# Two feed-forward chores exchanged between VectorE and GpSimd: weight sums of the down projection and sums of its activations

## The chip, the cores and the metric

The kernel runs on one core of a Trainium2 chip. The metric is device time in microseconds (us) of one execution; lower is better. TensorE does the matrix products, VectorE (DVE) and GpSimd (POOL) element-wise work, ScalarE (ACT) activations; SyncE (SP) issues the weight loads.

## The reference

Two transformer-like blocks of two layers each, in float32, on 256 tokens of width 1024. Between mixers (which the change leaves alone) stand six feed-forward stages, of which only these lines matter:

```python
# first block, 2 layers: d_ff = 4096
h @ mlp_w1  ->  square(relu(.))  ->  @ mlp_w2
# second block, 2 layers, two stages each: d_ff = 2816
(jax.nn.silu(h @ w_gate) * (h @ w_up)) @ w_down
```

So there are two plain stages and four gated ones, each with one or two projections in and one projection down.

## The kernel before

All weights are one stream of units of 128x1024 float32 (512 KB), loaded by SP into `ring`, which has 12 slots; TensorE hands slots back through `freed`, and SP then loads the next unit.

Each feed-forward (`Ffn`, `pe_ffn`, `act_ffn`, `dve_ffn`, `pool_ffn`) is a Strassen-like scheme with 7 products in place of 8 and has three parts.

- **Lead.** Four tiles of the hidden layer are computed directly.
- **Job phase.** Each job takes two ring units and makes seven products of 4 matmuls each. Four of its left operands are sums of weight blocks, which `in_sums` writes into `b.sums` (`HELD` = 4 buffers) with four instructions of 128x512: VectorE does the even jobs, GpSimd the odd ones. After each pair of hidden tiles (one job in a plain stage, two in a gated one) ScalarE copies one product out of PSUM (L543), VectorE joins the products (`join`, L584 to L593), in a gated stage ScalarE applies the SiLU (L550), and VectorE writes the activations to `hid_all` (L611 plain, L607 gated).
- **Down phase.** It goes over 16 pairs of hidden tiles (plain) or 11 (gated), 76 in all. Each pair takes two ring units, has seven products (`part` 1 to 7), and needs two things prepared. The *weight sums* (`down_sums`, four instructions of 128x512, L419, L420, L422, L424) go into the next of the same four `b.sums` buffers. The *inner-tile sums*, called activation sums here (four instructions of 128x128, L664, L665, L667, L669), go into `x_sums` in `cat`, also four buffers. A buffer comes free for pair p when TensorE has finished pair p - 4, counted by `job_done`.

TensorE asks for both before each pair, in `take`:

```python
def take(p):
    pe.wait_ge(*fn.summed(k, fn.jobs + p))          # weight sums
    pe.wait_ge(k.hid_summed, fn.down0 + p + 1)      # activation sums
```

The order of its work in the down phase is written out by hand. It first takes pairs 0 and 1 and runs parts 1, 6 and 5 of both, which need no bank that VectorE is still joining; then it waits for the last `joined`, and does parts 2, 3, 7, 4 of both. The middle pairs are done one after another. The last four pairs (`TAIL` = 4) are taken one after another with only part 1 between two takes; the other parts follow, each for all four pairs, so that the joins of the output can begin early.

Every engine works through its own queue in program order; semaphores are the only coupling.

Of the kernel before, what the change touches and what calls it, by code (L numbers as in the profile page):

```python
# [14 lines left out]
ALU = mybir.AluOpType  # L15
# [59 lines left out]
LEAD, TAIL, HELD = 4, 4, 4  # L75
# [23 lines left out]
class Steps:  # L99
# [5 lines left out]
    def __init__(self, sem, labels):  # L105
        labels = labels.split() if isinstance(labels, str) else labels
        assert len(set(labels)) == len(labels)
        self.sem, self.labels, self.marked = sem, labels, 0
# [27 lines left out]
def bc(ap, n):  # L136

    return ap.unsqueeze(1).to_broadcast([ap.shape[0], n, ap.shape[1]])
# [130 lines left out]
def half(tt):  # L269
    return slice(tt * P, tt * P + P)  # L270
# [80 lines left out]
class Ffn:  # L351
# [6 lines left out]
    def __init__(self, n):  # L358
        before = [self.shape(i) for i in range(n)]
        self.gated, self.tiles, self.ins, self.pairs, self.jobs, self.downs = self.shape(n)  # L360
        self.n, self.units = n, FFN_UNITS[n]
        self.lead0 = LEAD * n
        self.hid0 = sum(x[1] for x in before)
        self.job0 = sum(x[4] + x[5] for x in before)
        self.dve0 = sum(x[4] // 2 + x[5] for x in before)
        self.pool0 = sum(x[4] // 2 for x in before)
        self.down0 = sum(x[5] for x in before)
        self.pair0 = sum(x[3] for x in before)
        self.silu0 = sum(x[3] for x in before if x[0])
# [8 lines left out]
    def summed(self, k, i):  # L378

        if i >= self.jobs:  # L380
            return k.dve_summed, self.dve0 + self.jobs // 2 + i - self.jobs + 1
        return (k.pool_summed, self.pool0 + i // 2 + 1) if i % 2 else (k.dve_summed, self.dve0 + i // 2 + 1)

    def joined(self, i):
# [4 lines left out]
def unit_halves(k, eng, fn, i):  # L389

    out = []
    for j in range(2):
        u = fn.units + LEAD * fn.ins + 2 * i + j
        eng.wait_ge(k.filled[u % RING], 16 * (u // RING + 1))
        out += [k.ring[:, u % RING, 0:512], k.ring[:, u % RING, 512:1024]]
    return out


def in_sums(k, b, eng, fn, i, done):

    s = b.sums[:, i % HELD, :, :]
    if i >= HELD:
        eng.wait_ge(k.job_done, fn.job0 + i - HELD + 1)
    a11, a12, a21, a22 = unit_halves(k, eng, fn, i)
    eng.tensor_tensor(s[:, 0, :], a21, a22, ALU.add)  # L405
    eng.tensor_tensor(s[:, 2, :], a11, a21, ALU.subtract)
    eng.drain()
    eng.tensor_tensor(s[:, 1, :], s[:, 0, :], a11, ALU.subtract)
    eng.drain()
    eng.tensor_tensor(s[:, 3, :], a12, s[:, 1, :], ALU.subtract).then_inc(done, 1)  # L410


def down_sums(k, b, eng, fn, p, done):

    i = fn.jobs + p
    s = b.sums[:, i % HELD, :, :]
    eng.wait_ge(k.job_done, fn.job0 + i - HELD + 1)
    b11, b12, b21, b22 = unit_halves(k, eng, fn, i)
    eng.tensor_tensor(s[:, 0, :], b12, b11, ALU.subtract)  # L419
    eng.tensor_tensor(s[:, 2, :], b22, b12, ALU.subtract)  # L420
    eng.drain()
    eng.tensor_tensor(s[:, 1, :], b22, s[:, 0, :], ALU.subtract)  # L422
    eng.drain()
    eng.tensor_tensor(s[:, 3, :], s[:, 1, :], b21, ALU.subtract).then_inc(done, 1)  # L424
# [131 lines left out]
def dve_ffn(k, b, dve, fn, n_in, before_pairs=None):  # L556
    low, high = half(0), half(1)
    b11, b12, b21, b22 = k.h[:, 0:4, low], k.h[:, 0:4, high], k.h[:, 4:8, low], k.h[:, 4:8, high]
    hs = k.h_sums

    dve.wait_ge(k.h_low, 2 * n_in + 2)
    dve.drain()
    dve.tensor_tensor(hs[:, 0, :, :], b12, b11, ALU.subtract)
    dve.tensor_tensor(hs[:, 2, :, :], b22, b12, ALU.subtract)
    dve.drain()
    dve.tensor_tensor(hs[:, 1, :, :], b22, hs[:, 0, :, :], ALU.subtract)
    dve.drain()
    dve.tensor_tensor(hs[:, 3, :, :], hs[:, 1, :, :], b21, ALU.subtract).then_inc(k.tokens_summed, 1)
    in_sums(k, b, dve, fn, 0, k.dve_summed)
    for f in range(LEAD):  # L570
        dve.wait_ge(k.act_ready, fn.lead0 + f + 1)
        dve.tensor_tensor(b.hid_all[:, f, :], k.bank(4 + f)[:, int(fn.gated), :], k.hid_act[:, f % 2, :],
                          ALU.mult).then_inc(k.hid_ready, 1)
    in_sums(k, b, dve, fn, 2, k.dve_summed)
    if before_pairs is not None:
        before_pairs()

    def join(q):

        pre, i = b.pre[q % 2], q * fn.ins  # L580
        dve.wait_ge(k.first_copied, fn.pair0 + q + 1)
        for j in range(fn.ins):
            got, c = k.regions[:, (i + j) % 4, :, :], pre[:, j, :, :]
            dve.tensor_tensor(c[:, 0:5:4, :], bc(c[:, 7, :], 2), got[:, 1:3, :], ALU.add)  # L584
        dve.drain()
        for j in range(fn.ins):
            got, c = k.regions[:, (i + j) % 4, :, :], pre[:, j, :, :]
            dve.tensor_tensor(c[:, 5:7, :], bc(c[:, 4, :], 2), got[:, 4:6, :], ALU.add)
        dve.drain()
        for j in range(fn.ins):  # L590
            got, c = k.regions[:, (i + j) % 4, :, :], pre[:, j, :, :]
            dve.tensor_tensor(c[:, 1:4:2, :], c[:, 5:7, :], got[:, 3:5, :], ALU.add)
            last = dve.tensor_tensor(c[:, 2, :], c[:, 6, :], got[:, 6, :], ALU.subtract)  # L593
        last.then_inc(k.joined, 1)

    down = 0
    for q in range(fn.pairs):
        pre, f = b.pre[q % 2], LEAD + 2 * q
        out = b.hid_all[:, f:f + 2, :].rearrange("p n (h c) -> p (n h) c", c=P)
        join(q)  # L600
        ahead = (q + 1) * fn.ins + HELD
        for i in range(ahead - fn.ins, min(ahead, fn.jobs)):
            if i % 2 == 0:
                in_sums(k, b, dve, fn, i, k.dve_summed)
        if fn.gated:
            dve.wait_ge(k.silu_ready, fn.silu0 + q + 1)
            dve.tensor_tensor(out, k.silu[q % 2].rearrange("p (s c) -> p s c", c=P), pre[:, 1, 0:4, :],  # L607
                              ALU.mult).then_inc(k.hid_ready, 2)
        else:
            dve.drain()  # L610
            dve.scalar_tensor_tensor(out, pre[:, 0, 0:4, :], 0.0, pre[:, 0, 0:4, :], ALU.max, ALU.mult).then_inc(  # L611
                k.hid_ready, 2)
        while down < ahead - fn.jobs:
            down_sums(k, b, dve, fn, down, k.dve_summed)
            down += 1
    for p in range(down, fn.downs):
        down_sums(k, b, dve, fn, p, k.dve_summed)


def dve_join_first(k, dve, fn):  # L620
# [29 lines left out]


def pool_ffn(k, b, pool, fn, n_in):
    low, high = half(0), half(1)

    pool.wait_ge(k.y_done, 2 * n_in + 2)
    for i in range(1, fn.jobs, 2):
        in_sums(k, b, pool, fn, i, k.pool_summed)
    for p in range(fn.downs):
        x = k.x_sums[:, p % HELD, :, :]
        if p >= HELD:  # L660
            pool.wait_ge(k.job_done, fn.job0 + fn.jobs + p - HELD + 1)
        pool.wait_ge(k.hid_ready, fn.hid0 + 2 * p + 2)
        f1, f2 = b.hid_all[:, 2 * p, :], b.hid_all[:, 2 * p + 1, :]
        pool.tensor_tensor(x[:, 0, :], f1[:, high], f2[:, high], ALU.add)  # L664
        pool.tensor_tensor(x[:, 2, :], f1[:, low], f1[:, high], ALU.subtract)  # L665
        pool.drain()
        pool.tensor_tensor(x[:, 1, :], x[:, 0, :], f1[:, low], ALU.subtract)  # L667
        pool.drain()
        pool.tensor_tensor(x[:, 3, :], f2[:, low], x[:, 1, :], ALU.subtract).then_inc(k.hid_summed, 1)  # L669


def act_root_table(k, act):
# [572 lines left out]
def second_vector(k, s, dve, w):  # L1245
# [52 lines left out]
    for l in range(LAYERS):  # L1298
# [3 lines left out]
        dve.tensor_tensor(s.sg_wt.rearrange("p (h t) -> p h t", h=4), s.p("sg_w").rearrange("p (h t) -> p h t", h=4),  # L1302
                          bc(k.c("tril_st"), 4), ALU.mult)
        dve_ffn(k, s, dve, Ffn(2 + 2 * l), border(1, l, 0) - 1)
        dve_boundary(k, s, dve, 3 * l, "mix_pre_g", None, Ffn(2 + 2 * l))

# [167 lines left out]
        out_normed(1, 4)  # L1474
        dve_boundary(k, s, dve, 3 * l + 1, "ffn2_pre_g", lambda: out_gated(1))
        dve_ffn(k, s, dve, Ffn(3 + 2 * l), border(1, l, 1))
        if l < LAYERS - 1:
            dve.wait_ge(s.params, (l + 2) * 16)
# [1312 lines left out]
def tail_vector(k, f, s, dve, w, layer):  # L2791
    def norm(which, gain, bias):
# [3 lines left out]
        for tt in range(2):  # L2796
# [24 lines left out]
            last.then_inc(k.h_high, 1)  # L2821
    norm(LN1, "ln1_g", "ln1_b")
    dve_ffn(k, f, dve, Ffn(layer), border(0, layer, LN1), lambda: dve.wait_ge(f.residual, 2 * (2 * layer) + 2))
    norm(LN2, "ln2_g", "ln2_b")
    n = border(0, layer, PLE)
# [315 lines left out]
```

## Time and profile before

| | |
|---|---|
| time, median of 3 runs (lowest to highest) | 2066.53 us (2061.09 to 2070.67) |
| time of the profiled execution | 2056.4 us |
| its span, first to last instruction | 2054.6 us |
| mean granted TensorE clock | 0.984 of full speed |
| busy: PE, DVE, ACT, POOL | 98%, 53%, 17%, 31% of the span |
| chain that ended last | PE 92%, DVE 4%, ACT 1%, POOL 0% |

A busy share says how long an engine had an instruction running, not whether somebody waited for it. The chain that ended last is followed back from the last instruction, so an engine with a large share there sets the time. Shares are averages over unlike stages; what an exchange of work in one phase costs is read from the timeline of that phase. Each float32 matmul of the source appears as two records, so a down pair has 14 matmul records and a job 56.

### The profile page before, as it was taken

To read this page: it belongs to the slowest core of one execution; us is meant where nothing else is said; L and a number is where in the kernel's file an instruction comes from. 1 tells how busy PE (TensorE), PEld (TensorE's weight loads), DVE (VectorE), ACT (ScalarE), POOL (GpSimd) and SP (SyncE) were. 2 spreads that over 40 slices of the span, in tenths; PEclk is the share of its full clock that TensorE was granted. 3 is DMA by queue.
4 is the path that set the end of the run, shared out by engine and by line. 5 is a ranking of instruction groups with operands and counts; after the bars stand their busy time and mean duration, and the time that the engine had idled before them with its cause. 6 is when DMAs were issued, how large, how long until landed. Compare 5 with 4: busy or idle time off the path is not lost.

```text
span 2054.6 us, 31876 instructions
## 1 busy us (share of the span) xinstructions
PE 2004.0 (98%) x12016; PEld 1549.2 (75%) x12016; DVE 1088.1 (53%) x1959; ACT 345.4 (17%) x772; POOL 636.9 (31%) x665
## 2 busy tenths in 40 slices
PE   8999999999999999999999999999999999999998
PEld 6875995468769944699658869994899478869973
DVE  4343866434638655346636544665456636444564
ACT  1332000012420000300024511000200025310000
POOL 0000644310106453134412603434234405312342
PEclk9999999999999999999999989999999999989999
DMA  8422544443144444354435116544744344025453
GB/s 312 142 68 73 191 174 168 147 152 128 56 146 172 164 179 159 120 203 170 164 133 164 53 34 199 174 148 143 268 172 175 145 155 143 11 93 185 166 180 117
DMA packets 82935, 305.46 MB, mean 149 GB/s; under 512 B 9264, under 2 KB 9392, under 8 KB 82416
## 3 DMA queue, kind: packets, MB, share of 16 engines
q1 hardware_dynamic: 80496, 294.93, 40.9%
q0 software_dynamic: 2304, 8.65, 1.2%
q8 instruction: 95, 1.56, 0.3%
q14 instruction: 40, 0.33, 0.1%
HBM read 302.23 MB, written 1.05 MB: 148 GB/s over the span
## 4 chain that ended last, share of the span: by engine, by line
PE 92%; DVE 4%; ACT 1%; DVEq 1%; issue 1%; DMA 0%; POOL 0%; ACTq 0%; SPq 0%
PE psum L439 26%; PE psum L478 21%; PE psum L242 9%; PE psum L867 8%; PE psum L1814 6%; PE psum L2363 4%; PE psum L315 4%; PE psum L302 3%; PE psum L454 3%; PE psum L326 3%; PE psum L1673 1%; PE psum L451 1%; PE psum L283 1%; PE psum L2738 1%; PE psum L1751 0%
## 5 line engine op out<-in xcount | busy, mean ns | idle before, releaser
L439 PE MATMUL psum<-sq,space 128*128 128x128 f32 x2400 | 302.7, 276 | 0.0
L439 PEld LDWEIGHTS psum<-sq,space 128*128 128x128 f32 x2400 | 286.2, 193 | 0.0
L478 PE MATMUL psum<-space,cat 128*128 128x512 f32 x456 | 208.2, 592 | 0.0
L242 PE MATMUL psum<-h,ring 128*128 128x256 f32 x864 | 195.4, 386 | 7.0 <-DMA ring<-in_weights 7.0
L242 PEld LDWEIGHTS psum<-h,ring 128*128 128x128 f32 x864 | 166.7, 194 | 32.6 <-issue 9.7
L478 PEld LDWEIGHTS psum<-space,cat 128*128 128x128 f32 x456 | 86.4, 189 | 109.3 <-issue 109.3
L405 POOL TENSOR_TENSOR space<-ring 128x512 f32<-128x512 f32 x50 | 66.3, 1326 | 316.7 <-PE psum L439 265.4
L478 PE MATMUL psum<-ring,space 128*128 128x512 f32 x304 | 144.2, 594 | 6.8 <-DVE space L424 6.8
L664 POOL TENSOR_TENSOR cat<-space 128x128 f32<-128x128 f32 x76 | 59.6, 784 | 213.3 <-PE psum L478 213.3
L439 PE MATMUL psum<-sq,ring 128*128 128x128 f32 x800 | 107.7, 278 | 9.1 <-DVE space L410 9.1
L478 PEld LDWEIGHTS psum<-ring,space 128*128 128x128 f32 x304 | 56.7, 189 | 78.7 <-issue 66.4
L419 DVE TENSOR_TENSOR space<-ring 128x512 f32<-128x512 f32 x76 | 55.5, 731 | 107.9 <-PE psum L478 107.9
L439 PE MATMUL psum<-h,space 128*128 128x128 f32 x800 | 107.0, 277 | 0.0
L439 PEld LDWEIGHTS psum<-sq,ring 128*128 128x128 f32 x800 | 99.0, 195 | 9.4 <-DVE space L410 9.4
L439 PE MATMUL psum<-h,ring 128*128 128x128 f32 x800 | 105.7, 275 | 0.0
L584 DVE TENSOR_TENSOR tmp<-tmp,psum 128x256 f32<-128x256 f32 x68 | 26.8, 419 | 141.4 <-ACT tmp L543 141.3
L439 PEld LDWEIGHTS psum<-h,space 128*128 128x128 f32 x800 | 98.8, 194 | 0.0
L302 PEld LDWEIGHTS psum<-h,ring 128*128 128x128 f32 x832 | 94.6, 192 | 4.6 <-issue 1.9
L439 PEld LDWEIGHTS psum<-h,ring 128*128 128x128 f32 x800 | 97.4, 192 | 0.0
L302 PE MATMUL psum<-h,ring 128*128 128x128 f32 x832 | 96.1, 275 | 0.0
L315 PE MATMUL psum<-h,ring 128*128 128x128 f32 x832 | 94.4, 275 | 0.0
L315 PEld LDWEIGHTS psum<-h,ring 128*128 128x128 f32 x832 | 93.6, 192 | 0.0
(411 smaller groups left out, 3302.8 us busy)
## 6 DMA issues: line engine op xcount, KB each, us to landing
ring<-in_weights SPq DMA_DIRECT2D x552, 512.0 KB, 4.1
space<-in_rows POOLq DMA_DIRECT2D x8, 512.0 KB, 8.5
space<-in_gains POOLq DMA_DIRECT2D x6, 512.0 KB, 4.3
const<-in_consts SPq DMA_DIRECT2D x1, 1493.0 KB, 11.0
h<-in_x SPq DMA_DIRECT2D x1, 1024.0 KB, 4.8
x<-in_x_tok SPq DMA_DIRECT2D x1, 1024.0 KB, 15.3
out<-x SPq DMA_DIRECT2D x2, 512.0 KB, 2.6
space<-in_params POOLq DMA_DIRECT2D x2, 509.5 KB, 7.0
```

Source lines behind the costliest of these rows:

```text
L242: last = pe.matmul(out, unit[:, i, :], rhs[:, i, :], start=(i == 0), stop=(i == KD - 1), skip_group_check=True)
L302: ins = pe.matmul(out[:, half(0)], unit[:, i, :], k.h[:, i, half(0)], start=(i == 0), stop=(i == KD - 1), skip_group_check=True)
L315: last = pe.matmul(out[:, half(1)], unit[:, i, :], k.h[:, i, half(1)], start=(i == 0), stop=(i == KD - 1), skip_group_check=True)
L326: ins = pe.matmul(k.psum[:, 2 * tt + b, :], lhs(j)[:, half(tt)], unit[:, b * 512:b * 512 + 512], start=first and j == 0, stop=last and j = ...
L405: eng.tensor_tensor(s[:, 0, :], a21, a22, ALU.add)
L439: last = pe.matmul(out, weights(i), tokens(i), start=(i == 0), stop=(i == 3), skip_group_check=True)
L454: pe.matmul(out[:, 0, :], a[:, j, :], k.h[:, j, low], start=False, stop=(j == 3), skip_group_check=True)
L478: return pe.matmul(k.psum[:, bank, :], lhs, rhs, start=(p == 0), stop=(p == fn.downs - 1), skip_group_check=True)
L664: pool.tensor_tensor(x[:, 0, :], f1[:, high], f2[:, high], ALU.add)
L867: return pe.matmul(out, lhsT, rhs, start=start, stop=stop, skip_group_check=True)
L1814: return pe.matmul(out, lhsT, rhs, start=start, stop=stop, skip_group_check=True)
L2363: return pe.matmul(out, lhsT, rhs, start=start, stop=stop, skip_group_check=True)
```

## The change

Before, VectorE makes the weight sums of the down phase and GpSimd the activation sums. After, GpSimd makes the weight sums and VectorE the activation sums. In `dve_ffn` the loop that interleaved `down_sums` with the last joins is gone; the activation sums of all pairs stand behind the loop over hidden pairs, so behind the last join and the last activation. In `pool_ffn` `down_sums` stands where the activation sums stood. The counts on which TensorE waits are moved from `dve_summed` to `pool_summed`. TensorE's and ScalarE's programs are otherwise the same.

```diff
@@ class Ffn
-        self.dve0 = sum(x[4] // 2 + x[5] for x in before)
-        self.pool0 = sum(x[4] // 2 for x in before)
+        self.dve0 = sum(x[4] // 2 for x in before)
+        self.pool0 = sum(x[4] // 2 + x[5] for x in before)
@@ def summed
-            return k.dve_summed, self.dve0 + self.jobs // 2 + i - self.jobs + 1
+            return k.pool_summed, self.pool0 + self.jobs // 2 + i - self.jobs + 1
@@ def dve_ffn
-    down = 0
     for q in range(fn.pairs):
...
-        while down < ahead - fn.jobs:
-            down_sums(k, b, dve, fn, down, k.dve_summed)
-            down += 1
-    for p in range(down, fn.downs):
-        down_sums(k, b, dve, fn, p, k.dve_summed)
+    for p in range(fn.downs):
+        x = k.x_sums[:, p % HELD, :, :]
+        if p >= HELD:
+            dve.wait_ge(k.job_done, fn.job0 + fn.jobs + p - HELD + 1)
+        dve.drain()
+        f1, f2 = b.hid_all[:, 2 * p, :], b.hid_all[:, 2 * p + 1, :]
+        dve.tensor_tensor(x[:, 0, :], f1[:, high], f2[:, high], ALU.add)
+        dve.tensor_tensor(x[:, 2, :], f1[:, low], f1[:, high], ALU.subtract)
+        dve.drain()
+        dve.tensor_tensor(x[:, 1, :], x[:, 0, :], f1[:, low], ALU.subtract)
+        dve.drain()
+        dve.tensor_tensor(x[:, 3, :], f2[:, low], x[:, 1, :], ALU.subtract).then_inc(k.hid_summed, 1)
@@ def pool_ffn
     for p in range(fn.downs):
-        x = k.x_sums[:, p % HELD, :, :]
...
-        pool.wait_ge(k.hid_ready, fn.hid0 + 2 * p + 2)
...
-        pool.tensor_tensor(x[:, 3, :], f2[:, low], x[:, 1, :], ALU.subtract).then_inc(k.hid_summed, 1)
+        down_sums(k, b, pool, fn, p, k.pool_summed)
```

On VectorE, the end of the first feed-forward's job phase before: the join and activation of the last hidden pair (waiting for ScalarE's copy), then the weight sums of down pair 3, those of pairs 0 to 2 standing further up between earlier joins.

```order
L584 TENSOR_TENSOR tmp<-tmp,psum 128x2x128 [waits strassen_first_copied]
L588 TENSOR_TENSOR tmp<-tmp,psum 128x256
L592 TENSOR_TENSOR tmp<-tmp,psum 128x2x128
L593 TENSOR_TENSOR tmp<-tmp,psum 128x128
L611 SCALAR_TENSOR_TENSOR space<-tmp 128x512
L419 TENSOR_TENSOR space<-ring 128x512 [waits ring_filled6,ring_filled5,strassen_products]
L420 TENSOR_TENSOR space<-ring 128x512
L422 TENSOR_TENSOR space<-ring,space 128x512
L424 TENSOR_TENSOR space<-space,ring 128x512
```

On VectorE at the same place of the changed kernel (where L610 is the former L611), the four activation sums of pair 0 follow that last activation:

```order
L584 TENSOR_TENSOR tmp<-tmp,psum 128x2x128 [waits strassen_first_copied]
L588 TENSOR_TENSOR tmp<-tmp,psum 128x256
L592 TENSOR_TENSOR tmp<-tmp,psum 128x2x128
L593 TENSOR_TENSOR tmp<-tmp,psum 128x128
L610 SCALAR_TENSOR_TENSOR space<-tmp 128x512
L618 TENSOR_TENSOR cat<-space 128x128
L619 TENSOR_TENSOR cat<-space 128x128
L621 TENSOR_TENSOR cat<-cat,space 128x128
L623 TENSOR_TENSOR cat<-space,cat 128x128
```

So the activation sums that TensorE needs first have moved from an engine that ran beside the joins to a place behind the last of them.

On GpSimd, before, the last of its job sums is followed by activation sums that wait for `hidden_ready`:

```order
L405 TENSOR_TENSOR space<-ring 128x512 [waits ring_filled10,ring_filled9,strassen_products]
L406 TENSOR_TENSOR space<-ring 128x512
L408 TENSOR_TENSOR space<-space,ring 128x512
L410 TENSOR_TENSOR space<-ring,space 128x512
L664 TENSOR_TENSOR cat<-space 128x128 [waits hidden_ready]
L665 TENSOR_TENSOR cat<-space 128x128
L667 TENSOR_TENSOR cat<-cat,space 128x128
L669 TENSOR_TENSOR cat<-space,cat 128x128
```

On GpSimd after, the weight sums of pair 0 stand there and wait for a free buffer and for the ring:

```order
L405 TENSOR_TENSOR space<-ring 128x512 [waits ring_filled10,ring_filled9,strassen_products]
L406 TENSOR_TENSOR space<-ring 128x512
L408 TENSOR_TENSOR space<-space,ring 128x512
L410 TENSOR_TENSOR space<-ring,space 128x512
L419 TENSOR_TENSOR space<-ring 128x512 [waits ring_filled0,ring_filled11,strassen_products]
L420 TENSOR_TENSOR space<-ring 128x512
L422 TENSOR_TENSOR space<-ring,space 128x512
L424 TENSOR_TENSOR space<-space,ring 128x512
```

What moved here is the larger of the two chores: four instructions of 128x512 in place of four of 128x128 for each pair.

## Rows read from the trace of the kernel before

**Rows 1.** The page: busy time by engine, chain that ended last.
```profile
PE 2004.0 (98%) x12016; PEld 1549.2 (75%) x12016; DVE 1088.1 (53%) x1959; ACT 345.4 (17%) x772; POOL 636.9 (31%) x665
...
PE 92%; DVE 4%; ACT 1%; DVEq 1%; issue 1%; DMA 0%; POOL 0%; ACTq 0%; SPq 0%
```

**Rows 2.** Groups by line and shape, whole span; columns: busy us, mean ns | idle before.
```profile
L478 PE MATMUL psum<-ring,space 128*128 128x512 f32 x304 | 144.2, 594 | 6.8 <-DVE space L424 6.8
...
L664 POOL TENSOR_TENSOR cat<-space 128x128 f32<-128x128 f32 x76 | 59.6, 784 | 213.3 <-PE psum L478 213.3
...
L419 DVE TENSOR_TENSOR space<-ring 128x512 f32<-128x512 f32 x76 | 55.5, 731 | 107.9 <-PE psum L478 107.9
```

**Rows 3.** Timeline, steady down phase, first feed-forward: start us, us, instruction, [idle before <- releaser].
```profile
368.43 0.69 DVE L419 TENSOR_TENSOR space<-ring 128x512 f32<-128x512 f32 x1 [2.73 <-PE psum L478]
...
374.44 0.69 DVE L419 TENSOR_TENSOR space<-ring 128x512 f32<-128x512 f32 x1 [2.73 <-PE psum L478]
```

**Rows 4.** Timeline, first feed-forward, end of jobs, start of the down phase.
```profile
314.16 1.02 PE L478 MATMUL psum<-ring,space 128*128 128x512 f32 x2
...
314.67 0.42 DVE L584 TENSOR_TENSOR tmp<-tmp,psum 128x256 f32<-128x256 f32 x1 [1.12 <-ACT tmp L543]
...
316.00 0.28 DVE L593 TENSOR_TENSOR tmp<-tmp,psum 128x128 f32<-128x128 f32 x1
...
316.37 0.69 DVE L611 SCALAR_TENSOR_TENSOR space<-tmp 128x512 f32<-128x512 f32 x1
```

**Rows 5.** Timeline, fourth feed-forward (gated), the same place.
```profile
1379.00 1.02 PE L478 MATMUL psum<-ring,space 128*128 128x512 f32 x2
...
1379.62 0.75 DVE L584 TENSOR_TENSOR tmp<-tmp,psum 128x256 f32<-128x256 f32 x2 [2.76 <-ACT tmp L543]
...
1382.45 0.63 ACT L550 ACTIVATE hid<-tmp 128x512 f32<-128x512 f32 x1 [2.87 <-DVE tmp L593]
...
1383.18 0.69 DVE L607 TENSOR_TENSOR space<-hid,tmp 128x512 f32<-128x512 f32 x1 [0.77 <-ACT hid L550]
...
1383.79 0.68 DVE L419 TENSOR_TENSOR space<-ring 128x512 f32<-128x512 f32 x1
```

**Rows 6.** Timeline, first feed-forward: GpSimd's sum for one job, VectorE beside.
```profile
289.39 1.27 POOL L405 TENSOR_TENSOR space<-ring 128x512 f32<-128x512 f32 x1 [6.92 <-PE psum L439]
...
290.62 1.27 POOL L406 TENSOR_TENSOR space<-ring 128x512 f32<-128x512 f32 x1
...
291.36 1.08 DVE L611 SCALAR_TENSOR_TENSOR space<-tmp 128x512 f32<-128x512 f32 x1
...
292.04 1.53 POOL L408 TENSOR_TENSOR space<-space,ring 128x512 f32<-128x512 f32 x1
...
293.71 1.26 POOL L410 TENSOR_TENSOR space<-ring,space 128x512 f32<-128x512 f32 x1
294.93 0.46 POOL L664 TENSOR_TENSOR cat<-space 128x128 f32<-128x128 f32 x1
```

**Rows 7.** Timeline of GpSimd, first feed-forward: its first two sums, VectorE busy throughout.
```profile
225.49 1.72 POOL L405 TENSOR_TENSOR space<-ring 128x512 f32<-128x512 f32 x1
...
231.75 1.71 POOL L405 TENSOR_TENSOR space<-ring 128x512 f32<-128x512 f32 x1
...
236.70 1.53 POOL L410 TENSOR_TENSOR space<-ring,space 128x512 f32<-128x512 f32 x1
```

**Rows 8.** Timeline, first feed-forward: the last sums of the down phase.
```profile
386.46 0.69 DVE L419 TENSOR_TENSOR space<-ring 128x512 f32<-128x512 f32 x1 [2.73 <-PE psum L478]
386.50 0.96 POOL L664 TENSOR_TENSOR cat<-space 128x128 f32<-128x128 f32 x1 [2.46 <-PE psum L478]
...
388.95 0.78 DVE L424 TENSOR_TENSOR space<-space,ring 128x512 f32<-128x512 f32 x1
...
390.15 1.10 PE L478 MATMUL psum<-ring,space 128*128 128x512 f32 x2 [1.15 <-DVE space L424]
```

**Rows 9.** Timeline of TensorE: the first of two such gaps.
```profile
226.13 2.08 PE L439 MATMUL psum<-sq,ring 128*128 128x128 f32 x8 [4.51 <-DVE space L410]
```

**Rows 10.** Windows around such gaps: busy us of PE, PEld, DVE, ACT, POOL; PEclk, DMA, GB/s.
```profile
221.00:225.00 4.00, 0.62 (x6) 0.43 (x4) 3.93 (x2) 0.00 (x0) 3.86 (x2) 0.86 0.54 195
224.00:231.00 7.00, 4.87 (x24) 4.87 (x25) 6.75 (x8) 0.76 (x2) 6.72 (x5) 0.52 0.24 77
231.00:238.00 7.00, 7.00 (x66) 7.00 (x64) 6.78 (x8) 0.28 (x1) 6.72 (x5) 1.00 0.39 125
...
628.00:632.00 4.00, 4.00 (x20) 4.00 (x20) 3.82 (x5) 0.71 (x2) 3.72 (x4) 0.50 0.26 94
632.00:636.00 4.00, 4.00 (x32) 4.00 (x31) 3.74 (x4) 0.28 (x1) 4.00 (x3) 0.82 0.42 168
```

More of the change, by code:

```diff
@@ L652, in pool_ffn @@
 def pool_ffn(k, b, pool, fn, n_in):
-    low, high = half(0), half(1)
     pool.wait_ge(k.y_done, 2 * n_in + 2)
@@ L658, in pool_ffn @@
     for p in range(fn.downs):
-        x = k.x_sums[:, p % HELD, :, :]
-        if p >= HELD:
-            pool.wait_ge(k.job_done, fn.job0 + fn.jobs + p - HELD + 1)
-        pool.wait_ge(k.hid_ready, fn.hid0 + 2 * p + 2)
[L663 to L668, printed above, removed]
-        pool.tensor_tensor(x[:, 3, :], f2[:, low], x[:, 1, :], ALU.subtract).then_inc(k.hid_summed, 1)
+        down_sums(k, b, pool, fn, p, k.pool_summed)
 def act_root_table(k, act):
```

## The prediction

> **What bounds the kernel now.** The page first: TensorE is busy for 98% of the span and holds 92% of the chain that ended last [rows 1]. A microsecond in which TensorE stands still is therefore a microsecond of the kernel, and work that ends before TensorE asks for it costs nothing. So I look only for places where TensorE would wait.
>
> Next the groups by line [rows 2]. The down phase has 76 pairs. In all of them together TensorE stood idle 6.8 us before its matmuls, on VectorE's last weight sum (L424). GpSimd's activation sums are never what it waited for. Both helpers wait for TensorE instead (107.9 us before L419, 213.3 us before L664): they have room.
>
> Then the timeline of the first feed-forward. In the steady down phase a pair takes 374.44 - 368.43 = 6.01 us, 0.43 us for each of its 14 matmul records [rows 3]. This is the beat against which both helpers are measured. At the seam between job phase and down phase TensorE passes without a pause into pair 0 at about 314.05 (the rows begin at 314.16), while VectorE is still joining the last hidden pair: L584 starts at 314.67, L611 at 316.37 and ends at 317.06 [rows 4]. What covers the joins is parts 1, 6 and 5 of pairs 0 and 1, which need only early activations: 12 records, 5.2 us. In a gated stage the same stretch is longer, since the SiLU lies in between: TensorE starts the down phase at 1379.00, the SiLU at 1382.45, and L607 ends at 1383.87 [rows 5].
>
> **The change part by part.** There are four terms. The matmuls, the weight loads and ScalarE's work are the same.
>
> *1. The start of the down phase.* Activation sum 0 now stands on VectorE behind the last L611/L607, and TensorE's first take asks for it. The cover of 5.2 us is gone, because those 12 records themselves wait. Plain stage: L611 ends 3.0 us after TensorE's arrival. Then come four instructions of 128x128; one of that size takes 0.28 us [rows 4], and with the two drains I estimate 1.2 us for the four. From the end of the last weight sum to TensorE's restart 0.4 us pass (388.95 + 0.78 = 389.73 to the row at 390.15) [rows 8]. That makes 4.6 to 5.1 us if VectorE is undisturbed. It won't be. Job 13 being done also releases buffer 3, so GpSimd starts weight sum 3 in the same moment and works for 5.5 us. Beside a running GpSimd sum the L611 took 1.08 us in place of 0.69 us [rows 4, 6], and GpSimd's L408 after it took 1.53 us. Where both read SBUF with two inputs, one waits for the other. If each small instruction waits out one GpSimd instruction of 1.27 us until GpSimd has finished, sum 0 ends near 6.8 us and TensorE restarts near 7.2 us. I take 7.0 (bounds 5.1 and 7.5). Gated stage: L607 ends 4.9 us after the arrival (1383.87 - 1379.00) [rows 5]. With 1.2 and 0.4 that is 6.5 us, with up to 1.1 us for a GpSimd instruction in the way and some 0.6 us for a second 8.2; I take 7.3. Sum 1 follows some 1.1 us later, while TensorE has 2.6 us of work on pair 0, and hides. Term: 2 x 7.0 + 4 x 7.3 = **43.2 us** (36.2 to 47.8).
>
> The Trainium skill (SBUF — State Buffer, section "SBUF: two separate sides") says that VectorE with two SBUF inputs and GpSimd take a shared port pair by an exclusive lock, and that the loser blocks until the other's instruction ends. The trace agrees so far: 1.08 us for L611 in [rows 6]. Without the rule the term would be 36.2 us, with it about 47.
>
> *2. TensorE's clock after that pause.* The two longest waits inside feed-forward stages were 4.5 us each, before L439 (the first of them in [rows 9]). The granted clock fell to 0.5 (1.2 GHz) inside the first, and after the work resumed at 226.13 it stayed there until about 230.7: the window from 224 to 231 has 0.52, the next one 1.00. After the second, resumed at 627.6, it was 0.50 to 632 and 0.82 over the next 4 us, so low until about 633.4 [rows 10]. At half clock the matmuls ran at half rate, so 4.6 and 5.8 us of it cost 2.3 and 2.9 us. My pauses of 7 us are longer than those of 4.5 us, so I charge 2.6 us each: 6 x 2.6 = **15.6 us** (13.8 to 17.4).
>
> *3. The last weight sum of the phase.* Its buffer comes free when pair n - 5 is done, which is when TensorE starts taking the last four pairs with only part 1 between the takes. TensorE is back 2.6 us later, and everything beyond is a stall. Before, VectorE needed 386.46 to 389.73, and TensorE stood about 1.2 us [rows 8], six times in the kernel (the 6.8 us of [rows 2]). Now GpSimd needs its own sum there. Its job sum has the same four instructions: from 289.39 to the next instruction at 294.93 it took 5.54 us, with one L611 beside it [rows 6]. Without the stretch of L408 (1.53 against 1.27) it is 5.3 us. Beside a VectorE that is busy throughout, two sums took (236.70 + 1.53 - 225.49) / 2 = 6.4 us each [rows 7]. In the new steady phase the same semaphore releases VectorE's four small instructions and GpSimd's sum, so there is some contention, but of small instructions: I take 5.6 us. Against TensorE's restart 3.9 us after the release before, it now comes 0.25 + 5.6 + 0.4 = 6.25 us after it: 2.35 us more.
>
> This holds if GpSimd is free at the release. Counting from TensorE's delayed start, pair 0 is done after 20 records (8.6 us), and only then can GpSimd begin sum 4. A gated stage has seven sums from there (4 to 10): 8.85 + 7 x 5.6 = 48.05 us, against 42.1 + 0.25 + 5.6 = 47.95 without a backlog. So it is just worked off: 2.45 us. In a plain stage twelve sums end at 76.05, earlier than 78.0: no backlog. The sums in between are ready long before their pair, thanks to the four buffers, and cost nothing; the cover is three pairs of 6.01 us. Term: 2 x 2.35 + 4 x 2.45 = **14.5 us**. With 5.3 us it is 12.3; with 6.4 us, longer than a pair, backlog builds and the term is about 2 x 9.9 + 4 x 8.0 = 52.
>
> *4. The clock after that second pause.* TensorE's pause there grows from 1.2 to about 3.6 us. The clock did not fall at 1.2 us, and did at 4.5 us. I take half of the price: 6 x 1.3 = **8 us** (0 to 17).
>
> *What gets nothing.* The weight sums leave VectorE's late joins; but each L584 already waits for ScalarE and that for TensorE's products (1.12 and 2.76 us idle before it) [rows 4, 5], so an emptier VectorE gains nothing. GpSimd's later ring readers don't hold the ring: a slot is handed back by part 3, which comes after the take.
>
> Sum: 43.2 + 15.6 + 14.5 + 8 = 81 us. From the profiled execution's 2056.4 us it gives 2138 us. The median of the runs shown is 10 us above that execution, so the predicted median is **2148 us**, 3.9% slower.
>
> **The rivals.**
>
> *GpSimd becomes the beat (0.22).* If the port is held for a VectorE instruction's whole 0.28 us, the four add 1.1 us to a quiet sum of some 5.1 to 5.3 us: 6.25 to 6.4 us, more than the pair's 6.01. The lag then grows with every pair. With 6.25: plain 8.85 + 12 x 6.25 + 0.4 - 76.1 = 8.2 us, gated 8.85 + 7 x 6.25 + 0.4 - 46.0 = 7.0 us (76.1 and 46.0 are the restart before: 12 or 7 pairs of 6.01 us and the 3.9 us), so term 3 is 44 us in place of 14.5, and term 4 is due in full (16): 2186 us. For it: the 6.4 us of [rows 7]. Against it: these stood beside VectorE instructions four times as large. It decides at 6.01 us for a sum. This is the outcome that the exclusive lock of the Trainium skill (the same page and section) would give if it is held for whole small instructions; no row of before shows such small ones beside a large GpSimd one.
>
> *Contention and clock cost little (0.13).* VectorE gets the port first each time, so that term 1 is 36.2; term 2 is 13.8, term 3 12.3 and term 4 nothing: 62 us, about 2128 us. For it: L419 kept 0.69 us beside a GpSimd L664 [rows 3, 8]. Against it: L611's 1.08 us.
>
> *No slower (0.03).* The mechanism would be VectorE itself: freed of four large instructions for every pair, it ends the last join so early that activation sum 0 meets TensorE. For that the last L611 plus four small ones would have to end within the time of TensorE's arrival, against 3.0 + 1.2 us now, and GpSimd's last sum would have to take under 3.3 us. The time would be about 2065 us. Nothing speaks for it: the join can't start before the last job's products exist.
>
> **How the numbers follow.** The forecast has 0.62; its own range is 2130 to 2165. The range reaches down to the low-cost rival (with scatter of the runs, 2115) and up to the GpSimd rival (2190). A measurement of this kernel can tell about 0.5% (10 us) from no change. All cases but the last are slower by far more than this: slower 0.97, same 0.02, faster 0.01.
>
> **What would show it.** In the timeline after, at each seam: a gap of some 7 us of TensorE before L478, released by VectorE's L623; a granted clock of 0.5 for about 5 us behind it; in the groups, idle time of L478 near 40 us put down to VectorE and near 20 to GpSimd's L424; GpSimd's sum at 5.6 us with idle time before L419 in the steady phase; a pause near 3.6 us at the last take. I am wrong in term 1 if TensorE starts pair 0 without a gap. I am wrong in term 3 if GpSimd has no idle time between sums, or if TensorE stops at middle pairs. The job phase should keep its beat.

## The result, and the profile after

The changed kernel takes 2138.6 us (median of 4 runs, 2138.2 to 2143.4), the kernel before 2068.0 us beside it. The ratio is 1.0352, with a 95% interval of 1.0322 to 1.0382. The profiled execution has a span of 2136.8 us against 2054.6, so 82.2 us more. One execution in this study, of the first of the two kernels under "Only the first four activation sums moved", took 5334.1 us where its other three took 2129 to 2134; nothing here shows why, and its median and ratio below leave it out.

The page of the changed kernel, answering to [rows 1]: busy time by engine, then the chain that ended last.

```profile
PE 2034.8 (95%) x12016; PEld 1563.6 (73%) x12016; DVE 1167.9 (55%) x1959; ACT 345.6 (16%) x772; POOL 808.9 (38%) x665
...
PE 45%; issue 20%; POOLq 15%; POOL 15%; DVE 3%; ACT 1%; DMA 1%; DVEq 0%; ACTq 0%; SPq 0%
```

The share of GpSimd on the chain went from nothing to 30% with its sequencer. That invites the reading that GpSimd now sets the time. The experiments below show that it is a poor guide here.

The groups by line of the changed kernel, answering to [rows 2]: busy us, mean ns, then idle time before them and its releasers. L618 to L623 are the activation sums, now on VectorE.

```profile
L478 PE MATMUL psum<-ring,space 128*128 128x512 f32 x304 | 154.9, 630 | 58.6 <-POOL space L424 30.8 <-issue 27.9
...
L419 POOL TENSOR_TENSOR space<-ring 128x512 f32<-128x512 f32 x76 | 98.5, 1297 | 110.0 <-PE psum L478 94.0 <-PE psum L439 15.8
...
L618 DVE TENSOR_TENSOR cat<-space 128x128 f32<-128x128 f32 x76 | 79.4, 1045 | 67.4 <-PE psum L478 62.8 <-issue 0.7
```

TensorE's idle time ahead of the down matmuls grew from 6.8 to 58.6 us. It lies in twelve pauses, two for each feed-forward: one at the seam (6.43 us in a plain stage, 6.96 to 6.99 in a gated one; 40.7 us together), and one at the last take (3.10 and 2.93 us; 17.9 together). There is none elsewhere in the down phase. The second thing to see is the mean of L618: 1045 ns for an instruction of 128x128.

The timeline at the seam of the first feed-forward, answering to [rows 4]:

```profile
316.30 1.27 POOL L419 TENSOR_TENSOR space<-ring 128x512 f32<-128x512 f32 x1 [0.67 <-PE psum L439]
316.56 0.42 DVE L584 TENSOR_TENSOR tmp<-tmp,psum 128x256 f32<-128x256 f32 x1 [3.47 <-ACT tmp L543]
...
317.52 1.27 POOL L420 TENSOR_TENSOR space<-ring 128x512 f32<-128x512 f32 x1
...
318.26 1.07 DVE L610 SCALAR_TENSOR_TENSOR space<-tmp 128x512 f32<-128x512 f32 x1
318.93 1.52 POOL L422 TENSOR_TENSOR space<-ring,space 128x512 f32<-128x512 f32 x1
319.43 1.17 DVE L618 TENSOR_TENSOR cat<-space 128x128 f32<-128x128 f32 x1
320.52 0.28 DVE L619 TENSOR_TENSOR cat<-space 128x128 f32<-128x128 f32 x1
320.60 1.33 POOL L424 TENSOR_TENSOR space<-space,ring 128x512 f32<-128x512 f32 x1
320.88 1.20 DVE L621 TENSOR_TENSOR cat<-cat,space 128x128 f32<-128x128 f32 x1
322.14 0.29 DVE L623 TENSOR_TENSOR cat<-space,cat 128x128 f32<-128x128 f32 x1
...
322.65 2.05 PE L478 MATMUL psum<-ring,space 128*128 128x512 f32 x2 [6.43 <-POOL space L424]
```

L618 and L621 each lasted until 0.15 us after a GpSimd instruction ended (at 320.45 and 321.93); L610, which began beside L420, took 1.07 us in place of 0.69. L619 and L623 began where GpSimd had nothing running, and took 0.28 and 0.29 us. TensorE restarts 0.2 us after L623. The row names GpSimd's L424 as the releaser, but that sum is for pair 3 and ended at 321.93; what TensorE waited for was activation sum 0. In the four gated stages the profile names no releaser at all ("issue"); there too TensorE restarts 0.2 us after L623. The restart itself already runs at half clock: two records in 2.05 us, against 1.02 in [rows 4].

Windows over that place and over the last take of the same stage, answering to [rows 10] (the last three columns are granted clock, DMA share, GB/s):

```profile
318.00:322.00 4.00, 0.00 (x0) 0.00 (x0) 3.74 (x5) 0.00 (x0) 3.64 (x3) 0.73 0.00 0
322.00:327.00 5.00, 4.35 (x6) 2.00 (x7) 3.69 (x14) 0.00 (x0) 0.00 (x0) 0.54 0.02 5
327.00:332.00 5.00, 5.00 (x13) 2.13 (x12) 0.00 (x0) 0.00 (x0) 0.00 (x0) 1.00 0.00 0
402.00:406.00 4.00, 3.36 (x4) 1.51 (x5) 0.54 (x1) 0.69 (x2) 0.40 (x1) 0.50 0.00 0
```

Read window by window in this way, the low clock lasts 4.0 to 5.9 us of work after each of the six seam pauses, 31.2 us together, so 15.6 us lost at half rate. After the pauses at the last take it is low after four of six, 15.0 us together, 7.5 us lost.

The timeline at the last take, answering to [rows 8]:

```profile
397.05 1.27 POOL L419 TENSOR_TENSOR space<-ring 128x512 f32<-128x512 f32 x1 [0.66 <-PE psum L478]
397.07 1.39 DVE L618 TENSOR_TENSOR cat<-space 128x128 f32<-128x128 f32 x1 [0.53 <-PE psum L478]
398.27 1.31 POOL L420 TENSOR_TENSOR space<-ring 128x512 f32<-128x512 f32 x1
398.39 1.35 DVE L619 TENSOR_TENSOR cat<-space 128x128 f32<-128x128 f32 x1
399.73 1.26 POOL L422 TENSOR_TENSOR space<-ring,space 128x512 f32<-128x512 f32 x1
399.81 1.33 DVE L621 TENSOR_TENSOR cat<-cat,space 128x128 f32<-128x128 f32 x1
401.13 1.26 POOL L424 TENSOR_TENSOR space<-space,ring 128x512 f32<-128x512 f32 x1
401.21 1.33 DVE L623 TENSOR_TENSOR cat<-space,cat 128x128 f32<-128x128 f32 x1
402.64 1.19 PE L478 MATMUL psum<-ring,space 128*128 128x512 f32 x1 [3.10 <-POOL space L424]
```

GpSimd's sum takes 5.34 us with four VectorE instructions beside it (5.2 us in a gated stage, from 1076.50 to 1081.68), hardly more than its quiet length. It is VectorE that pays: each small instruction waits out one GpSimd instruction, so the activation sum takes as long as the weight sum and even ends last, at 402.54 against 402.39. TensorE's restart is 0.1 us behind it. And GpSimd had 0.66 us of idle time before the sum: the steady phase holds its beat of 6.01 us.

### The profile page after: what moved, and what is told of

It is laid out like the page before. It is cut to its first block, busy times and chain, and to the rows that moved or that the text cites. A ratio compares the mean times of both kernels' runs of the same rounds, so it can differ in the third digit from the quotient of the medians.

```text
span 2136.8 us, 31900 instructions
## 1 busy us (share of the span) xinstructions
PE 2034.8 (95%) x12016; PEld 1563.6 (73%) x12016; DVE 1167.9 (55%) x1959; ACT 345.6 (16%) x772; POOL 808.9 (38%) x665
## 4 chain that ended last, share of the span: by engine, by line
PE 45%; issue 20%; POOLq 15%; POOL 15%; DVE 3%; ACT 1%; DMA 1%; DVEq 0%; ACTq 0%; SPq 0%
PE psum L242 9%; PE psum L862 7%; PE psum L1809 6%; PE psum L478 6%; POOLq L423 5%; POOLq L421 5%; POOL space L420 5%; POOL space L424 4%; PE psum L2358 4%; PE psum L315 4%; PE psum L302 3%; POOL space L410 3%; POOLq L407 3%; POOL space L406 3%; PE psum L326 2%
## 5 line engine op out<-in xcount | busy, mean ns | idle before, releaser
L478 PE MATMUL psum<-space,cat 128*128 128x512 f32 x456 | 221.5, 623 | 0.0
L478 PE MATMUL psum<-ring,space 128*128 128x512 f32 x304 | 154.9, 630 | 58.6 <-POOL space L424 30.8
L242 PEld LDWEIGHTS psum<-h,ring 128*128 128x128 f32 x864 | 167.1, 195 | 32.7 <-issue 9.6
L405 POOL TENSOR_TENSOR space<-ring 128x512 f32<-128x512 f32 x50 | 65.5, 1310 | 312.5 <-PE psum L439 261.7
L478 PEld LDWEIGHTS psum<-space,cat 128*128 128x128 f32 x456 | 92.1, 202 | 120.8 <-issue 120.8
L478 PEld LDWEIGHTS psum<-ring,space 128*128 128x128 f32 x304 | 59.8, 201 | 134.2 <-issue 108.6
L419 POOL TENSOR_TENSOR space<-ring 128x512 f32<-128x512 f32 x76 | 98.5, 1297 | 110.0 <-PE psum L478 94.0
L618 DVE TENSOR_TENSOR cat<-space 128x128 f32<-128x128 f32 x76 | 79.4, 1045 | 67.4 <-PE psum L478 62.8
L439 PE MATMUL psum<-h,ring 128*128 128x128 f32 x800 | 105.7, 275 | 0.0
L422 POOL TENSOR_TENSOR space<-ring,space 128x512 f32<-128x512 f32 x76 | 99.5, 1309 | 10.8
L420 POOL TENSOR_TENSOR space<-ring 128x512 f32<-128x512 f32 x76 | 100.7, 1325 | 0.0
L302 PEld LDWEIGHTS psum<-h,ring 128*128 128x128 f32 x832 | 94.6, 192 | 4.6 <-issue 1.9
L439 PEld LDWEIGHTS psum<-h,ring 128*128 128x128 f32 x800 | 97.4, 192 | 0.0
L424 POOL TENSOR_TENSOR space<-space,ring 128x512 f32<-128x512 f32 x76 | 92.0, 1210 | 11.4 <-issue 0.9
```

Source lines behind the costliest of these rows:

```text
L242: last = pe.matmul(out, unit[:, i, :], rhs[:, i, :], start=(i == 0), stop=(i == KD - 1), skip_group_check=True)
L302: ins = pe.matmul(out[:, half(0)], unit[:, i, :], k.h[:, i, half(0)], start=(i == 0), stop=(i == KD - 1), skip_group_check=True)
L439: last = pe.matmul(out, weights(i), tokens(i), start=(i == 0), stop=(i == 3), skip_group_check=True)
L478: return pe.matmul(k.psum[:, bank, :], lhs, rhs, start=(p == 0), stop=(p == fn.downs - 1), skip_group_check=True)
```

## The experiments

The kernels ran in two batches, beside which the kernel before took 2063.4 and 2060.8 us, not 2068.0. Differences to the changed kernel are therefore given by the ratios (0.001 is 2.1 us; each has an interval of some 0.003) as well as by medians.

The theory is that of the prediction: the exchange costs two pauses of TensorE for each feed-forward and the low clock behind them, and the first comes from the place of activation sum 0 behind the last join. The rival that the chain of waits suggests: GpSimd is too slow for the weight sums, wherever the rest stands.

**The first four activation sums ahead of the last join** (`act_sums` holds the loop body of the change).

```diff
     for q in range(fn.pairs):
...
-    for p in range(fn.downs):
...
+        if fn.pairs - 1 - HELD <= q < fn.pairs - 1:
+            act_sums(q - (fn.pairs - 1 - HELD))
+    for p in range(HELD, fn.downs):
+        act_sums(p)
```

> The changed kernel, with the activation sums of down pairs 0 to 3 written by VectorE one each behind the activations of the four hidden pairs before the last, so ahead of the last join; everything else as changed. My theory (most of the loss is TensorE waiting at the seam for activation sum 0 behind the last join, and the clock that falls in that wait): the six gaps of 6.4 to 7.0 us before L478 and the half clock behind them (15.6 us in all by the trace) go, which leaves about 2138.6 - 41.6 - 15.6 = 2081 us, with the pause of about 3 us at the last take unchanged. Rival (GpSimd's weight sums are what costs, wherever the activation sums stand): 2130 us or more.

Measured: 2077.5 us, ratio 1.0083 (1.0052 to 1.0115) to the kernel before. The two windows over the seam show TensorE busy throughout, at full clock, with GpSimd still making weight sums:

```profile
305.00:315.00 10.00, 10.00 (x76) 8.72 (x75) 8.14 (x16) 0.56 (x2) 8.51 (x7) 1.00 0.52 189
315.00:325.00 10.00, 10.00 (x24) 4.37 (x23) 4.36 (x4) 0.00 (x0) 6.57 (x6) 1.00 0.36 116
```

By the ratios 56 us of the 73 are gone (1.0352 less 1.0083), by the medians 61, where 57 were expected, by moving 16 small instructions in each feed-forward. The rival falls as the account of the main loss. What is left fits the pauses at the last take, which this trace has at the same 2.93 to 3.11 us.

**A filler in the pause.**

```diff
     pe.wait_ge(k.joined, fn.joined(fn.jobs - fn.ins - 1))
+    flat_h = k.h.rearrange("p n t -> p (n t)")
+    for _ in range(7):
+        pe.matmul(k.psum[:, 4, :], k.h[:, 0, low], flat_h[:, 0:512], start=True, stop=True, skip_group_check=True)
     for p in range(2):
         take(p)
```

> The changed kernel, with 7 matmuls of 128x512 that nobody reads (14 records, 6.0 us, into the bank that part 1 of pair 0 overwrites) on TensorE ahead of its first take; the output is the same. It keeps TensorE busy in the wait without shortening it. My theory: the wait for activation sum 0 ends at the same time, the granted clock stays at 1.0 there, and 15.6 us come back: 2123 us. Rival (the low clock costs nothing because something else is late there): 2138 us. If the filler itself delays the start, 2130 us or more, with TensorE's gap gone.

Measured: 2123.6 us, ratio 1.0304 (1.0273 to 1.0336). That is 15.0 us less than the changed kernel by the medians, 14.7 by the profiled spans (2122.1), but only 10 by the ratios, whose intervals overlap a little. The timeline of TensorE at the same seam:

```profile
314.96 6.17 PE L483 MATMUL psum<-h 128*128 128x512 f32 x14
321.47 1.10 PE L478 MATMUL psum<-ring,space 128*128 128x512 f32 x2 [0.33 <-issue]
```

The wait is still there, filled with work that nobody reads; the first two records now take 1.10 us and not 2.05. In the windows the clock is at 1.00 after each of the six waits. The low clock is a cost of its own apart from the pause, 10 to 15 us. The figure may be low by a few microseconds: two waits of the job phase, which the edit doesn't touch, were 12.7 us long together in this execution and 7.4 us in that of the changed kernel.

**Both chores on VectorE, GpSimd idle in the down phase.** This is the kernel before without the loop in `pool_ffn`, with `act_sums(0..3)` directly behind the last activation and `act_sums(p)` behind each later `down_sums`.

```diff
+        if q == fn.pairs - 1:
+            for p in range(HELD):
+                act_sums(p)
         while down < ahead - fn.jobs:
...
-    for p in range(down, fn.downs):
+    for p in range(HELD, fn.downs):
         down_sums(k, b, dve, fn, p, k.dve_summed)
+        act_sums(p)
```

> The kernel before, with the activation sums on VectorE too, those of pairs 0 to 3 behind the last activation, those of the others each behind the weight sum of its pair; GpSimd has no work in the down phase. My theory: what counts is the place behind the last join, and GpSimd's part of the loss is small. Start gaps of 4.3 us (plain) and 6.1 us (gated), 33 us together, 12 to 15 us of clock, about 1 us more at each last take: 2121 us. The small instructions take 0.29 us each, in place of the 1.2 to 1.4 us that they take beside GpSimd. Rival (the loss comes from GpSimd, by its slow sums or by its hold on the port): at most 2078 us.

Measured: 2108.4 us, ratio 1.0219 (1.0190 to 1.0249). The seam pauses are 4.27 and 6.24 to 6.27 us, close to the 4.3 and 6.1 expected, the activation sum's instructions 0.28 to 0.29 us each (L603 is the first of them):

```profile
L603 DVE TENSOR_TENSOR cat<-space 128x128 f32<-128x128 f32 x76 | 22.2, 292 | 7.0
```

The pauses at the last take are 1.71 us, with full clock behind all six. The total was expected some 13 us too high, 5 of them because the kernel before ran at 2063.4 in this batch and not at 2068. In this kernel no weight sum is late at the seam (the last one ended 5.0 us before TensorE's restart), and TensorE still restarts 0.21 us after the last instruction of activation sum 0, as in the changed kernel; at the last take it is 0.10 us in both. That confirms which sum is waited for. So most of the pause at the seam is place (4.27 of 6.43 us, 6.24 of 6.96 us); GpSimd's presence adds 2.2 us in a plain stage and 0.7 in a gated one.

**Only the first four activation sums moved, weight sums as before.** Two kernels, both the kernel before with GpSimd's loop begun at pair 4 (where it first waits for VectorE's four sums). The first has:

```diff
+    for p in range(HELD):
+        act_sums(p)
     for p in range(down, fn.downs):
         down_sums(k, b, dve, fn, p, k.dve_summed)
```

> The kernel before with one thing of the change: the activation sums of down pairs 0 to 3 are made by VectorE behind the last activation; all others stay on GpSimd and all weight sums on VectorE. My theory: this alone gives the start term without GpSimd in the way, gaps of 4.3 us (plain) and 6.1 us (gated), 33 us, and some 14 us of low clock: 2115 us; the last take stays at 1.2 us. Rival (who makes the weight sums is what costs): 2068 us, as before.

Measured: 2133.7 us (3 runs), ratio 1.0336 (1.0297 to 1.0375), 19 us more than expected. The trace tells why: at this place of the code the sums stand behind the weight sum of pair 3 too (2 and 3 in a gated stage), which the loop of the last join had queued. The pauses are 7.00 and 11.72 us, which is 4.27 and 6.24 plus one and two weight sums of some 2.74 us. My edit was not the one that the expectation describes, and the miss shows once more that TensorE waits for whatever stands ahead of activation sum 0. The edit as meant puts the four calls ahead of the `while`, as in the kernel above:

> As the kernel e7, but with the activation sums of pairs 0 to 3 directly behind the last activation and the weight sums of pair 3 (2 and 3 in a gated stage) behind them, as e7 was meant to be. My theory: start gaps of 4.27 us (plain) and 6.24 us (gated), 33.5 us, with 12 to 14 us of low clock behind them, nothing else: 2063 + 46 = 2109 us, like the kernel with both chores on VectorE. Rival (the weight sums' maker decides): 2063 us.

Measured: 2114.8 us, ratio 1.0249 (1.0219 to 1.0280), with pauses of 4.27, 4.28 and 6.24 to 6.38 us, and 29.7 us of work at half clock behind them. The profile's list of TensorE's waits (us together, times, longest) has them in one line:

```profile
PE psum L478 <- issue: 33.7, 6, 6.4
```

Expected were 2109 us. With every weight sum still on VectorE, more than two thirds of the whole loss is there (0.0249 of 0.0352).

**A later wait at the last pair.**

```diff
     for p in last_pairs:
-        take(p)
+        if p < fn.downs - 1:
+            take(p)
+        else:
+            units[p] = pe_take(k, pe, w), pe_take(k, pe, w)
         last = part(1, p)
...
+            if name == 6 and p == fn.downs - 1:
+                pe.wait_ge(*fn.summed(k, fn.jobs + p))
+                pe.wait_ge(k.hid_summed, fn.down0 + p + 1)
             last = part(name, p)
```

> The changed kernel; at the last pair of each down phase TensorE takes the ring units and runs part 1, which reads no sum, and waits for the two sums only ahead of part 6 of that pair, six records (2.6 us) later. My theory: the pause of 2.93 to 3.10 us at the last take shrinks to about 0.4 us and its clock loss (7.5 us in the trace of the changed kernel) goes, since no pause so short was followed by a low clock: 2138.6 - 6 x 2.6 - 7.5 = 2115.5 us. Rival (GpSimd's late sum only moves the pause to a later part): 2138 us.

Measured: 2109.6 us, ratio 1.0233 (1.0204 to 1.0263): less than the changed kernel by 25 us by the ratios, 29 by the medians, where 23 were expected. No pause at the last take is left in the trace; the six seam pauses stand unchanged (6.44 and 6.96 us).

**Both repairs.**

> Both repairs together on the changed kernel: activation sums of pairs 0 to 3 ahead of the last join, and the late wait of TensorE at the last pair. If the two pauses are all that the exchange costs, this kernel is at 2077.5 - 15.6 = 2062 us or less, as fast as the kernel before within the measurement, although GpSimd makes every weight sum. Rival (the exchange has a further cost, by contention on the joins or in the steady phase): 2072 us or more.

Measured: 2055.6 us (10 runs) where 2062 or less was expected, ratio 0.9966 (0.9945 to 0.9987). There is no idle time before L478 anywhere in its trace:

```profile
L478 PE MATMUL psum<-ring,space 128*128 128x512 f32 x304 | 142.8, 592 | 0.0
```

With GpSimd making every weight sum, this kernel is no slower than the one before, and by its interval slightly faster. But the later wait is an advantage that the kernel before doesn't have; the fair comparison is the next kernel, which has it too.

**The later wait on the kernel before.**

> The kernel before with the late wait of TensorE at the last pair alone. Its pause of 1.12 to 1.16 us (six times) is covered by six records: 6.8 us less, a ratio of 0.997 to the kernel before. Rival: no difference, because the join of the output sets the end of the phase anyway.

Measured: 2054.2 us (12 runs), ratio 0.9953 (0.9934 to 0.9972), the best kernel of the study, though not to be told from the one with both repairs (0.9953 against 0.9966, medians 1.4 us apart). So the exchange as such, contention included, costs nothing measurable once TensorE doesn't wait at these two places. The stalls of some 1.15 us of [rows 8] are gone. Its gain is 10 us by the ratio and 7 by the medians, where 7 were expected; the interval includes 7.

## Why the prediction was right

The median predicted was 2148 us, measured 2138.6; the sum was 81 us of addition to the profiled span, and the spans differ by 82.2. By terms:

| term | predicted | in the trace of after |
|---|---|---|
| 1, pause at the seam | 43.2 | 40.7 |
| 2, low clock behind it | 15.6 | 15.6 |
| 3, longer pause at the last take | 14.5 | 11.1 (17.9 less the 6.8 of before) |
| 4, low clock behind that | 8 | 7.5 |

*Term 1.* The mechanism was right, and was shown by moving the sums (56 to 61 us gone, terms 1 and 2 together), and by bringing both terms back without the exchange (51 us by the ratio, 54 by the medians). Estimated 7.0 and 7.3 us, measured 6.43 and 6.96: the latency from the last sum to TensorE's restart was 0.2 us, not the 0.4 that I took from [rows 8], and in a plain stage sum 0 ended 6.2 us after TensorE's arrival, not near 6.8, since only two of its four instructions waited out one of GpSimd's. The split was nearly right too: 4.27 and 6.24 us without GpSimd, where the estimates for an undisturbed VectorE were 4.6 to 5.1 and 6.5. The sign that I gave for it in the profile didn't come: no idle time was put down to VectorE's L623, but 30.8 us to GpSimd's L424 and 27.9 to "issue".

*Term 2.* The filler shows it alone, at 10 to 15 us. That the sum agrees to the tenth is luck: the single stretches run from 4.0 to 5.9 us.

*Term 3* was mis-sized by 3.4 us, most of it in its duration for GpSimd's sum. I took 5.6 us; it was 5.34 and 5.2. I had charged the contention to GpSimd, while VectorE bears it. Most of the rest is the latency: TensorE restarted 0.25 us after the weight sum, where I had taken 0.4. At the last take VectorE's activation sum was then as late as the weight sum, which I had not foreseen; it ended only 0.15 us behind.

*Term 4* was a half chance for each pause, and four of six came true.

The four terms by the trace make 75 us. The other 7 of the 82 lie in work that the change doesn't touch, where the clock was low for longer in this execution than in that of before: TensorE's busy time for the same 12016 instructions grew by 30.8 us (2034.8 less 2004.0), of which 23.1 are terms 2 and 4. In the first mixer, the same 18 us of before and of after (in this order):

```profile
85.00:103.00 18.00, 18.00 (x113) 16.25 (x113) 6.38 (x33) 4.28 (x8) 0.00 (x0) 0.81 0.50 163
```

```profile
85.00:103.00 18.00, 18.00 (x96) 16.54 (x95) 5.69 (x32) 4.11 (x7) 0.00 (x0) 0.62 0.43 146
```

0.19 of the clock over 18 us is 3.4 us. The two medians differ by 70.6 us, less than the two profiled spans, which agrees with this. It also means that my total was a few microseconds high and met the span partly by that accident; against the medians, 81 stands beside 70.6. I had also raised the forecast by the 10 us between the profiled execution of before and its median; the changed kernel's profiled execution was at its median.

*The rivals.* GpSimd as the beat did not come: from 5.34 us to 6.01 there is 0.66 us of idle time at each pair, as the row at 397.05 shows. The low-cost rival was off in both contention (term 1 at 36.2, measured 40.7) and clock (13.8 and nothing, measured 15.6 and 7.5). The total alone would hardly have told it from the forecast: its 62 us and the forecast's 81 are about equally far from the 70.6 between the medians. The trace agrees with the exclusive lock in the Trainium skill (SBUF — State Buffer, "SBUF: two separate sides") in that the loser waits until the other's instruction has ended (1.33 us for a VectorE instruction that takes 0.29 alone). It doesn't bear out what I made of it as a rival, that four small instructions would lengthen GpSimd's sum by their full duration.

## What to carry to other kernels

When two chores are exchanged between engines, ask first what each stands behind in its new queue at the moment when the critical engine asks for it, and only then how long it takes there: here the place of a chore of 1.2 us (four small instructions) cost far more than doubling the duration of the larger one, which had three pairs of buffers to hide in. Count a new pause of a busy TensorE twice where it is as long as those of 3 us and more here, once as time and once as the low clock behind it. A wait that stands earlier than its first reader is worth moving even in a kernel that looks full: part 1 needed neither sum, and moving the last wait six records down made the kernel before faster too.

## What the runs showed of the hardware

- After a pause of TensorE of 4.27 us or more at the seam of the down phase the clock was at its lower level in all 30 cases of five traces (in one it fell 0.7 us after the restart). After those of 2.92 to 3.11 us at the last take it was in 9 of 18 (three traces), and in two more it fell 1.4 us after the restart. After those of 1.1 to 1.7 us there it was in none of 24 (four traces). Where it was low, the work ran at half clock for 2.9 to 6.1 us. Length alone doesn't decide: a pause of 1.64 us near the end of the first mixer (restart at 155.41 in the changed kernel) was followed by the lower level within 1.2 us in 8 of the 10 traces.
- Where GpSimd's instructions of 128x512 with two SBUF inputs and VectorE's of 128x128 run in step, VectorE's grow from 0.29 to 1.33 us, one whole GpSimd instruction, while GpSimd's stay at 1.26 to 1.31 us. In [rows 8], with large VectorE and small GpSimd instructions, the small GpSimd ones grew most (L664 0.96 us against 0.46 in [rows 6]); of the large VectorE ones L419 kept its 0.69 us and L424 took 0.78. In both the short ones paid the larger share.
- The releaser named for a pause was GpSimd's L424, where VectorE's L623 came later and was the one waited for. The chain's 30% for GpSimd is of the same kind: with both repairs the whole loss was gone and GpSimd's share of the chain was 2%, with the same weight sums on GpSimd at the same speed (L419 at 1301 ns, 1297 in the changed kernel).
